# The first expert group's rows from a product with a one-hot table, instead of a gather

## The reference

```python
def routed_moe(x, router_w, router_b, w_gate, w_up, w_down):
    xt = x.reshape(B * S, D)
    aff = jax.nn.sigmoid((xt @ router_w).astype(jnp.float32))
    sel = aff + router_b.astype(jnp.float32)
    ...
    _, e_idx = lax.top_k(jnp.where(e_mask, sel, -jnp.inf), TOPK_EXPERTS)
    w = jnp.take_along_axis(aff, e_idx, axis=1)
    w = w / jnp.sum(w, axis=-1, keepdims=True)
    ...
    for e in range(N_EXPERTS):
        h = jax.nn.silu(xt @ w_gate[e]) * (xt @ w_up[e])
        y = y + gates[:, e:e + 1] * (h @ w_down[e])
```

## Time and profile before

| | |
|---|---|
| time, median of 3 runs | 2001.99 us |
| the profiled execution's own time | 2001.53 us |
| its span | 1999.9 us |
| granted TensorE clock, mean of the span | 0.972 of full |
| PE busy | 1906.5 us, 95% |
| DVE busy | 655.7 us, 33% |
| ACT busy | 409.1 us, 20% |
| POOL busy | 84.9 us, 4% |
| layer 0: PE's first expert product starts, its group of 128 rows lasts | 1108.16 us, 16.23 us |
| layer 1: the same | 1694.79 us, 16.46 us |
| a later group's gate and up products | 13.87 us |

### The profile page before, as it was taken

The page is one execution under the profiler, slowest core; times in us unless marked ns, Lnnn a source line. Parts: engine busy times, 40 slices in busy tenths (PEclk is TensorE's granted clock), DMA queues, the critical chain, the costliest instruction groups (busy, mean ns, idle before and its releaser), DMA issues.

```text
span 1999.9 us, 23138 instructions
## 1 busy us (share of the span) xinstructions
PE 1906.5 (95%) x9746; PEld 878.9 (44%) x9746; DVE 655.7 (33%) x1579; ACT 409.1 (20%) x874; POOL 84.9 (4%) x107
## 2 busy tenths in 40 slices
PE   6999999999999999999997899999999996999997
PEld 3464464444444444644545333333644644333332
DVE  3746232223310043114615200003598645100005
ACT  3213011111100002113621111111326701111112
POOL 0000100000000000000000200001000000200001
PEclk9989999999999999999997899999998996999999
DMA  3201921122211221310133599999112134799994
GB/s 146 84 22 63 376 97 61 65 84 73 84 35 70 74 77 42 126 43 1 43 148 143 193 401 415 421 416 338 42 43 85 43 138 147 254 421 415 419 400 164
DMA packets 74121, 335.70 MB, mean 168 GB/s; under 512 B 6632, under 2 KB 15864, under 8 KB 61600
## 3 DMA queue, kind: packets, MB, share of 16 engines
q1 hardware_dynamic: 59872, 283.91, 36.8%
q0 software_dynamic: 10976, 37.78, 5.1%
q10 hardware_dynamic: 3168, 12.50, 1.5%
HBM read 311.07 MB, written 23.09 MB: 167 GB/s over the span
## 4 chain that ended last, share of the span: by engine, by line
PE 92%; DVE 4%; ACT 1%; issue 1%; DMA 1%; DVEq 0%; SPq 0%; ACTq 0%
PE psum L623 37%; PE psum L1111 26%; PE psum L905 8%; PE psum L832 5%; PE psum L1006 3%; PE psum L1039 2%; PE psum L1019 2%; PE psum L982 2%; PE psum L1093 1%; PE psum L1206 1%; PE psum L635 1%; PE psum L1137 1%; PE psum L774 1%; ACT ring L1564 1%; PE psum L1266 1%
## 5 line engine op out<-in xcount | busy, mean ns | idle before, releaser
L1111 PE MATMUL psum<-ring,scratch 128*32 128x512 f32 x3840 | 518.0, 599 | 5.8 <-issue 2.3
L623 PE MATMUL psum<-xT,ring 128*128 128x512 f32 (+1 forms) x1184 | 452.1, 542 | 6.1 <-PE psum L623 3.9
L623 PEld LDWEIGHTS psum<-xT,ring 128*128 128x128 f32 x1184 | 223.4, 190 | 231.4 <-issue 223.6
L1111 PEld LDWEIGHTS psum<-ring,scratch 128*32 128x32 f32 x3840 | 142.8, 111 | 295.8 <-issue 287.1
L623 PE MATMUL psum<-ring,xT 128*128 128x512 f32 (+2 forms) x512 | 196.7, 541 | 0.6 <-PE psum L623 0.3
L905 PE MATMUL psum<-ring,scratch 128*128 128x512 f32 x352 | 152.8, 594 | 1.8 <-PE psum L905 1.5
L1735 DVE SCALAR_TENSOR_TENSOR scratch<-psum,overlay,scratch 128x511 f32<-128x511 f32 x88 | 65.9, 749 | 220.6 <-ACT scratch L1496 219.0
L623 PEld LDWEIGHTS psum<-ring,xT 128*128 128x128 f32 x512 | 91.7, 190 | 99.6 <-issue 91.4
L1111 PE MATMUL psum<-xT,scratch 128*32 128x512 f32 x768 | 127.0, 594 | 0.0
L2274 DVE TENSOR_TENSOR scratch<-psum,scratch 128x512 f32<-128x512 f32 x24 | 16.6, 691 | 316.3 <-PE psum L1111 316.3
L905 PEld LDWEIGHTS psum<-ring,scratch 128*128 128x128 f32 x352 | 66.3, 190 | 86.9 <-issue 86.9
(11 more groups left out here) (379 smaller groups left out, 1650.0 us busy)
## 6 DMA issues: line engine op xcount, KB each, us to landing
ring<-in_moe_w_gate SPq DMA_DIRECT2D x28, 2048.0 KB, 10.9
ring<-in_moe_w_up SPq DMA_DIRECT2D x28, 2048.0 KB, 13.1
ring<-in_moe_w_down SPq DMA_DIRECT2D x24, 2048.0 KB, 12.1
ring<-in_w_up SPq DMA_DIRECT2D x11, 2048.0 KB, 9.0
xT<-in_moe_w_down SPq DMA_DIRECT2D x8, 2048.0 KB, 11.2
expert_rows<-scratch ACTq DMA_DIRECT2D x20, 512.0 KB, 10.6
ring<-in_w_down SPq DMA_DIRECT2D x4, 2048.0 KB, 7.7
ring<-in_even_w_in SPq DMA_DIRECT2D x4, 2048.0 KB, 8.7
```

Source lines behind the costliest of these rows:

```text
L623: mm = nc.tensor.matmul(out_, lhsT, rhs, start=(j == 0), stop=(j == len(pairs) - 1))
L1111: mm = nc.tensor.matmul(bank[r, :], lhsT[:, t, r], w_[:, t, c0:c0 + 512], start=(t == 0), stop=(t == nk - 1))
```

## The change

Group 0 of each layer is no longer gathered. From the ranks, DVE makes `first_slot`, each token's slot plus one in expert order (0 if the rank is 96 or more), for each of its two choices, and from that `first_hot`, four tables of 128 tokens by 128 slots: 1 where one of the token's two slots is that slot. It lies in the second half of `late_hot`. PE multiplies x by it in 32 products of 128x128, each over 128 tokens and 128 columns of x, four accumulating into one block of 128x128. The result is group 0's rows, already turned, in banks 0 and 1. These products stand between the rank products and the list products. POOL gathers groups 1 to 11; the gather of group 2 waits for nothing any more. The `count_up` table is one longer.

```diff
+                pe.wait_ge(hot_ready, 3 * l + 1)
+                for h in range(2):
+                    for t in range(4):
+                        mm = product(banks[h][:, t * P:(t + 1) * P],
+                                     [(of_partition[:, n, 4 * h + t, :], first_hot[:, n, :]) for n in range(NT)])
+                    mm.then_inc(xgT_done, 1)
                 for j in range(2):
-                    pe.wait_ge(hot_ready, 2 * l + j + 1)
+                    pe.wait_ge(hot_ready, 3 * l + j + 2)
...
-                turn_x(l, 0)
...
+                step(V.scalar_tensor_tensor(flat(first_slot), flat(rank_of), 1.0, flat(first_place), ALU.add, ALU.add))
+                step(V.scalar_tensor_tensor(flat(first_slot), flat(rank_of), float(CAP), flat(first_slot), ALU.is_lt, ALU.mult))
+                from_one = operand["count_up"][:, 1:P + 1]
+                begun_hot = [begun(V.tensor_scalar(first_hot[:, n, :], from_one, first_slot[:, 0, n:n + 1], None, ALU.is_equal))
+                             for n in range(NT)]
+                for n in range(NT):
+                    finished(begun_hot[n])
+                    ins = V.scalar_tensor_tensor(first_hot[:, n, :], from_one, first_slot[:, 1, n:n + 1], first_hot[:, n, :],
+                                                 ALU.is_equal, ALU.add)
+                ins.then_inc(hot_ready, 1)
...
-                for g in range(NG):
-                    if g >= 2:
+                for g in range(1, NG):
+                    if g >= 3:
```

More of the change, by code:

```diff
@@ L104, in packs @@
         ("over_need", rows(np.array([CAP + k * P for k in range(OVER_K) for e in range(E)], f))),
-        ("count_up", rows(np.arange(P, dtype=f))),
+        ("count_up", rows(np.arange(P + 1, dtype=f))),
         ("expert_of", rows(np.tile(np.arange(E, dtype=f), NT))), ("group_of", rows(np.tile(np.arange(4, dtype=f), NT))),
@@ L593, in build @@
         late_share = ar.take(2 * NT, 2)
+        first_hot, first_slot = late_hot[1].rearrange("p (n q) -> p n q", q=P), ar.take(2, NT)
         here_weight = ar.take(2, NT)
@@ L1073, in route @@
                 flat = lambda a: a.rearrange("p a b -> p (a b)")
+                of_partition = x.rearrange("q n (p k) -> q n k p", k=KD)
                 pe.wait_ge(chosen_ready, l + 1)
@@ L1089, in turn_x @@
                 of_partition = xg[:, g % 2, :].rearrange("q (p k) -> q k p", k=KD)
-                pe.wait_ge(gathered[g % 2], 16 * (NG // 2 * l + g // 2 + 1))
+                pe.wait_ge(gathered[g % 2], 16 * ((NG // 2 - 1 + g % 2) * l + (g + 1) // 2))
                 for h in range(2):
@@ L2216, in route @@
                 for j in range(2):
-                    V.tensor_tensor(at_rank[:, j], operand["count_up"].unsqueeze(1).to_broadcast([P, NT, P]),
+                    V.tensor_tensor(at_rank[:, j], operand["count_up"][:, 0:P].unsqueeze(1).to_broadcast([P, NT, P]),
                                     place_f[:, j, :].unsqueeze(2).to_broadcast([P, NT, P]), ALU.is_equal).then_inc(hot_ready, 1)
@@ L2296, in seek_late @@
                     step(V.tensor_tensor(late_hot[g].rearrange("p (n q) -> p n q", q=P),
-                                         operand["count_up"].unsqueeze(1).to_broadcast([P, NT, P]),
+                                         operand["count_up"][:, 0:P].unsqueeze(1).to_broadcast([P, NT, P]),
                                          late_row[:, g, :].unsqueeze(2).to_broadcast([P, NT, P]), ALU.is_equal))
```

## The result

The changed kernel is slower: 2012.32 us median (2007.31 to 2016.19, six runs) against 2001.09 us for the kernel before (six runs), a ratio of 1.0056 with a 95% interval of 1.0042 to 1.0071, that is 8.4 to 14.2 us. The forecast was 1997.3 us.

What follows compares the result with a forecast made beforehand. The prediction took PE as the bound, with the experts' start and slow-clocked first group deciding. Layer gains of 2.11 and 2.20 us made 4.3 off 2001.53, so 1997.2; it said 1997.3 us, 8-in-10 range 1994.0 to 2003.0.

Steps and rivals of the forecast that it cites:

- The product's rows: 64 rows between rank and list products: 0.224 us each at half clock, 0.114 at full, 9.66 us, nothing added for step.
- The rival that named this: In the product, stationary loads at a step cost double: 9.7 us more per layer, 2016.6 us in all; chance 3%.
- The clock's rise inside the product: Within the 64 rows the clock goes from 0.50 to 1.00 after 4.8 us of dense work.
- the rival of a clock that never rises: Through the 64 rows the clock stays low: product 14.3 us, experts 6.6 us later, 2014.9 us; chance 9%.
- DVE ahead of the product: Between rank sums and product, two slot steps 0.42 us, four comparisons 0.64, four sums 0.89, handing over 0.05.
- The list products as cover: Behind the product, 16 list products take 1.85 us at high clock and cover ACT's copy of the turned rows.
- The clock's gain in the first group: First expert group runs at full clock, winning 2.36 us in layer 0 and 2.59 in layer 1.
- the rival of 13%: Between product and experts the clock falls again or comes too late; first group stays slow, 2002.1 us; chance 13%.
- What moves behind: Behind the product, `place_tokens` ends at 1119.7 with 2.6 us slack; gathers of groups 1 and 2 land in time.

Runs made afterwards that it cites:

- the probe: The kernel before plus measured stretches of 32 products or transposes on constants at various steps behind the last norm; its time was not meant to count.
- the runs without the step: The changed kernel with neighbouring columns of x as stationary operand (0.9970 of before), or with x first copied apart by ScalarE (0.9980).
- the second run of the changed kernel: The changed kernel unaltered, run again on the experiments' chip beside the kernel before: 2003.44 us, ratio 1.0049.
- The filled kernel with 8, 5 and 9: The kernel before plus dense 128x256 products: 8 ahead of the rank products, 5 behind them, 9 behind the list products; 1980.14 us, ratio 0.9939.
- the run without the step: The changed kernel with 128 neighbouring columns of x as stationary operand, giving group 0 another column order: 1985.41 us, 0.9970 of before.
- the two kernels with the copy apart: The changed kernel with x copied by ScalarE into neighbouring floats: 1988.04 us, 0.9980 of before; with fillers of 8 and 3 added: 1981.01 us, 0.9946.
- six spare products: The kernel before plus six dense 128x256 products on constants behind the list products, during the first gather: 1986.74 us, ratio 0.9970.

## Why the prediction was wrong

- **The product's rows** ("The stationary operand is x at a step of 8 floats ... I add nothing"): this is the step that failed. I held the step to be free because the transposes of `xg` load with it and cost nothing. The reading of those rows was right, and the probe repeats it (3.54 against 3.42 us). What it did not allow was to carry them from a transpose to a product: in a product the step doubles a row at full clock, 0.24 instead of 0.114 us. 64 rows took 15.56 and 15.53 us instead of 9.66. That is 5.9 us a layer, 11.8 in sum, against a forecast gain of 4.3. The rival that named this had 3%, and was priced at 9.7 us a layer, because I doubled the rows at half clock as well; there the step costs next to nothing (0.24 against 0.22).
- **The clock's rise inside the product** was right in each run that had it start low. Without the step the product took 9.79, 10.04, 8.76 and 9.84 us, against 9.66. One reading behind the rival of a clock that never rises was too broad: among the attention products of 1523 to 1530 those of L1019 are 128*128, so not all of them use half of the array.
- **DVE ahead of the product**: 2.42 us instead of 2.03. The four comparisons took 0.87 instead of 0.64 us, the four sums 1.14 instead of 0.89. Some 0.8 us in the sum of both layers.
- **The list products as cover** for ACT's copy: right, 1.85 us at the high clock, and the experts followed at once.
- **The clock's gain in the first group**: right in size (13.94 us where it held) in the runs without the step and in both layers of the second run of the changed kernel. In the profiled run the clock fell again behind the product, so the rival of 13% was real there, and PE had no gap at that place (busy for 2.00 of 2.00 us from 1116 to 1118). What decides between the two was not settled.
- **What moves behind**: right. In layer 0 `place_tokens` ended at 1129.72 and the transposes of group 1 began at 1135.16 without a wait for a gather.
- With the product at 0.24 us a row and DVE at 2.42, the sum of the same steps for a run in which the clock holds is 2.42 + 15.5 + 1.7 = 19.6 us from reduction to experts, 6.3 more than before, less 2.3 in the first group: 4.0 a layer. The stretch of the second run shows 34.8 - 30.8 = 4.0.

By its timed ratio that run is 7.6 to 12.2 us slower than before, its stretches alone give 7.9, and its profiled execution (2000.32) lies 3.1 us under its median. The filled kernel with 8, 5 and 9 gains 9.4 to 14.7 us in time and 8.7 in its stretches, so at least 0.7 us is left open. The traces show where else time differs. From the second stretch to the end all eight traces of the experiments beside the probe's take 282.9 us. Between the stretches six take 549.4 to 549.9, the run without the step 547.3 and the changed kernel again 552.8. The 3.3 us more of the latter are not a mark of the change: the two kernels with the copy apart, which have its product too, are among the six, and on the first chip it is 556.0 us before and 555.1 changed. Ahead of the first stretch, where only fillers and ScalarE's copies were added, the eight take anything from 1092.9 to 1099.0 us, so single executions differ there by up to 6 us.

## What to carry to other kernels

Before a transposed copy is replaced by a product that reads the untransposed rows in place, look at the distance of neighbouring elements in both operands: for float32 products of 128 columns at full clock a step of 4 or more in the stationary operand doubled the row, and so did a step of 8 in the moving one, while transposes did not pay and 512 columns hid it. A price must be taken from the same kind of instruction, and if the trace has the shape only in another kind, that is a bound and not a price. And where a stage ends in a slow clock, try filling its waits first: six spare products brought as much as the rebuilt stage. Fit the filler to the wait at the clock that it will run at: 2.84 us of it in the 4.8 us of a gather let the clock fall again, and 5.82 us of it held the stage up.

## What the runs showed of the hardware

- Transposes don't pay for a step of 8 floats (3.54 against 3.42 us for 31 loads), products do (15.71 against 7.34 for 64). Why was not tried.
- A row with the stationary operand at a step of 8 takes 0.24 us at either clock level (6.4 or 3.7 us of low clock in a product of 15.56 or 15.53 us), so a higher clock gives nothing back.
- The clock can fall while PE is busy throughout. In the probe, products of 12 columns run from 2177.3 to 2186.7, behind dense work, and the clock fell from 1.00 to 0.50 among them. The 1.85 us of such products behind the table product did not bring it down in the second run of the changed kernel.

```profile
2176.00:2182.00 6.00, 6.00 (x47) 5.27 (x46) 0.00 (x0) 0.00 (x0) 0.00 (x0) 1.00 0.00 0
2183.00:2187.00 4.00, 4.00 (x17) 3.71 (x18) 0.00 (x0) 0.00 (x0) 0.00 (x0) 0.50 0.00 0
```
